# Second norm of the latent tiles between the context's q, k, v products; context pooling beside the latent projections

## The reference

```python
h = modulate(rms_norm(x, lp['g_ff1']), sh1, sc1)
x = x + 0.5 * g1 * swiglu(h, lp['w_ff1_in'], lp['w_ff1_out'])
h = modulate(rms_norm(x, lp['g_mix']), sh2, sc2)          # the second norm
proj = h @ lp['w_in']                                     # p, q, k, v and gate logits
q = rms_norm(q per head, lp['q_gain']); k = rms_norm(k per head, lp['k_gain'])
a = pool_mixer(p, lp['w_pool'], lp['pool_scale']) @ lp['w_br_pool']
b = attention(q, k, v) @ lp['w_br_att']    # context: dense; latent: 8x16 neighbourhood + cached keys
x = x + g2 * ((sig_A * a + sig_B * b) @ lp['w_out'])
h = modulate(rms_norm(x, lp['g_ff2']), sh3, sc3)
x = x + 0.5 * g3 * swiglu(h, lp['w_ff2_in'], lp['w_ff2_out'])
```

## Time and profile before

| | us |
|---|---|
| median of 3 runs | 1688.76 (1687.05 to 1701.29) |
| the profiled execution's own time | 1701.97 |
| its span on the slowest core (core 3) | 1700.4 |
| spans of the eight cores | 1680.7 to 1700.4 |
| PE busy, core 3 | 1536.0 (90%) |
| DVE, ACT, POOL busy, core 3 | 956.5, 494.2, 158.2 |

### The profile page before, as it was taken

How to read it: one execution, slowest core, us unless ns; L and a number is a source line. 1 busy time by engine, 2 the same in 40 slices (tenths; PEclk the granted TensorE clock), 3 DMA queues, 4 the chain that set the end, 5 groups by cost and what they waited for, 6 DMA issues and landing times.

```text
span 1700.4 us, 25281 instructions; the slowest of 8 cores (1680.7 to 1700.4 us)
## 1 busy us (share of the span) xinstructions
PE 1536.0 (90%) x8548; PEld 695.4 (41%) x8548; DVE 956.5 (56%) x1646; ACT 494.2 (29%) x739; POOL 158.2 (9%) x235
## 2 busy tenths in 40 slices
PE   1689999999999995698889888999999999999998
PEld 1234444444444442243434444444334444444443
DVE  2256556555566554464546665345366666666666
ACT  2651110111111125745636566235421111111110
POOL 2131000000000012300000000021210000000000
PEclk9799999999999997787889899999999999999999
DMA  9906442345432332457225355584322222222005
GB/s 183 243 1 91 75 67 37 48 74 76 75 48 43 59 87 99 101 116 142 37 56 120 99 113 113 138 186 75 50 38 38 37 38 38 38 38 38 13 1 198
DMA packets 35788, 134.68 MB, mean 79 GB/s; under 512 B 5072, under 2 KB 5200, under 8 KB 33616
## 3 DMA queue, kind: packets, MB, share of 16 engines
q0 software_dynamic: 22560, 79.88, 30.3%
q1 hardware_dynamic: 13104, 53.18, 9.3%
HBM read 191.95 MB, written 20.97 MB: 125 GB/s over the span
## 4 chain that ended last, share of the span: by engine, by line
PE 79%; DVE 6%; issue 5%; ACT 4%; DMA 4%; POOL 1%; DVEq 0%; ACTq 0%; SPq 0%; POOLq 0%
PE ps L413 76%; ACT arena L422 3%; DVE arena L430 3%; PE ps L410 3%; DMA arena<-wts 3%; DVE arena L426 2%; POOL arena L603 1%; DMA arena<-xin 1%; DVE arena L436 1%; ACT L422 1%; DVEq L183 0%; DVE arena L445 0%; DVE arena L442 0%; ACTq L183 0%; POOL arena L323 0%
## 5 line engine op out<-in xcount | busy, mean ns | idle before, releaser
L413 PE MATMUL ps<-arena 128*128 128x512 bf16 (+3 forms) x7108 | 1476.7, 363 | 132.9 <-DVE arena L430 53.5
L413 PEld LDWEIGHTS ps<-arena 128*128 128x128 bf16 x7108 | 646.7, 100 | 919.6 <-issue 336.8
L430 DVE SCALAR_TENSOR_TENSOR arena<-ps,arena 128x512 f32<-128x512 f32 (+2 forms) x860 | 562.5, 714 | 89.6 <-ACT arena L422 47.1
L422 ACT ACTIVATE arena<-ps 128x512 f32<-128x512 f32 (+4 forms) x418 | 266.1, 652 | 1045.8 <-PE ps L413 526.7
L426 DVE TENSOR_TENSOR arena<-arena,ps 128x512 bf16<-128x512 f32 (+1 forms) x198 | 130.2, 658 | 411.7 <-PE ps L413 382.4
L426 DVE TENSOR_TENSOR arena<-arena 128x512 f32<-128x512 f32 (+10 forms) x196 | 141.6, 738 | 114.9 <-ACT arena L422 89.3
L323 POOL DMA_DIRECT2D arena<-wts x150 | 79.9, 536 | 1255.5 <-PE ps L413 1025.0
L422 ACT ACTIVATE arena<-arena 128x512 bf16<-128x512 f32 (+6 forms) x230 | 165.6, 748 | 86.9 <-DVE arena L426 25.0
L410 PE MATMUL ps<-arena 128*128 128x65 bf16 (+3 forms) x1440 | 80.6, 214 | 25.5 <-DVE arena L436 16.0
L603 POOL TENSOR_TENSOR arena<-arena 128x512 bf16<-128x512 f32 (+3 forms) x77 | 75.9, 1010 | 186.4 <-ACT arena L422 99.3
L410 PEld LDWEIGHTS ps<-arena 64*128 64x128 bf16 (+1 forms) x1440 | 53.5, 98 | 79.0 <-issue 69.8
(11 more groups left out here) (12 smaller groups left out, 6.1 us busy)
## 6 DMA issues: line engine op xcount, KB each, us to landing
arena<-wts POOLq DMA_DIRECT2D x150, 512.0 KB, 8.8
arena<-xin SPq DMA_DIRECT2D x8, 1024.0 KB, 13.6
xspill<-arena SPq DMA_DIRECT2D x4, 2048.0 KB, 7.0
arena<-xspill SPq DMA_DIRECT2D x4, 2048.0 KB, 14.7
yoT<-arena SPq DMA_DIRECT2D x32, 256.0 KB, 2.3
arena<-ebias SPq DMA_DIRECT2D x12, 640.0 KB, 5.1
arena<-ebias SPq DMA_DIRECT2D x8, 768.0 KB, 5.4
nkT<-arena SPq DMA_DIRECT2D x8, 256.0 KB, 2.9
```

What stands on the lines that cost most here:

```text
L413: return P.emit("pe", lambda e: e.matmul(out, lhsT=lhsT, rhs=rhs, start=start, stop=stop), reads=reads, writes=writes, inc=inc)
L422: return P.emit("act", lambda e: e.activation(out=out, in_=in_, func=func, **kw), reads=reads, writes=writes)
L430: return P.emit("dve", lambda e: e.scalar_tensor_tensor(out=out, in0=in0, scalar=scalar, in1=in1, op0=op0, op1=op1), reads=reads, writes=w ...
```

## The change

Nothing is computed otherwise; instructions are issued in another order, on other engines and into other banks.

- The norms of tiles 2, 3 and 4 are no longer issued in stage I. `pump` stops at them, and `mixer` weaves all three between the context's q, k and v products (46 units of products against 78 pieces). All their squares go to POOL, and every second modulation to DVE (`sq="p"`, `mo="av"`). The norms of tiles 0 and 1 stay in stage I, with 6 of 8 squares on POOL and two pieces after a down product instead of three.
- For x of tiles 2 and 3 to stay in place during this, the memory is exchanged: context q, k, v now lie over x of tiles 0 and 1, latent k, v over tiles 2 and 3, and `x_reload` brings each tile back to the other pair's place.
- `p_gen(0)` moves from stage II to stage III, woven with the latent products.
- Banks: these norms' sums always take bank 4, so down products beside them, and in the last block of both feed-forward phases, rotate over three banks instead of four; the context products over four instead of six; the latent products over two (4, 5) instead of three, as bank 6 goes to `p_gen(0)`.

```diff
@@ build_program: order of the weight loads
-        for nm in ("q", "k", "p", "v"):
+        for nm in ("q", "k", "v"):
             plan_win(0, nm)
-        for nm in ("q", "k", "v"):
-            plan_win(1, nm)
+        plan_win(1, "q")
+        plan_win(0, "p")
+        plan_win(1, "k")
+        plan_win(1, "v")
@@ norm_stat, norm_gen
-        def norm_stat(tile):
+        def norm_stat(tile, bank=None):
-            b = poolB.next()
+            b = poolB.next() if bank is None else bank
...
-            b = stat if stat is not None else norm_stat(tile)
+            b = stat if stat is not None else norm_stat(tile, 4 if gap else None)
@@ ff_DN
-        def ff_DN(Dn, rd, nj, tile, hs, ig, ms=range(8), chunk_done=None):
+        def ff_DN(Dn, rd, nj, tile, hs, ig, ms=range(8), chunk_done=None, spare=False):
-                by = poolDN.next()
+                by = (poolDN3 if spare else poolDN).next()
...
         poolDN = PsumPool(P, [4, 5, 6, 7], "DN")
+        poolDN3 = PsumPool(P, [5, 6, 7], "DN3")
@@ ff_phase
             def pump(k):
-                while k > 0 and side:
+                while k > 0 and side and not (lazy_load is not None and side[0][0] > 1):
...
-                                  chunk_done=chunk_done if last else None)
-                            pump(3 if last else 2)
+                                  chunk_done=chunk_done if last else None, spare=bool(side) or last)
+                            pump(2)
@@ x_reload
-            claim_x(tt)
+            XT[tt] = XT0[tt ^ 2]
+            dst = XT[tt].rearrange("p c t -> p (c t)")
+            P.claim(oX[tt ^ 2], 16384, [("x", c, tt) for c in range(8)])
...
-        QT = (mem(oX[2], 8192, BF16, "p (h t) -> p h t", h=4), mem(oS, 8192, BF16, "p (h t) -> p h t", h=4))
+        QT = (mem(oX[0], 8192, BF16, "p (h t) -> p h t", h=4), mem(oS, 8192, BF16, "p (h t) -> p h t", h=4))
...
@@ mixer
-            while left and left[0][0] <= 2:
+            while left and left[0][0] < 2:
                 run_all(left.pop(0)[1])
...
-            d1, s1 = PsumPool(P, [0, 1, 2, 3, 4, 5], "d1"), PsumPool(P, [6, 7], "s1")
-            weave(qk_gen(0, "q", d1, s1), 16.0, side, 40.0)
...
-            weave(chain_gens(qk_gen(0, "k", d1, s1), v_gen(0, d1)), 30.0, p_gen(0, d1), 21.0)
+            d1, s1 = PsumPool(P, [0, 1, 2, 3], "d1"), PsumPool(P, [6, 7], "s1")
+            weave(chain_gens(qk_gen(0, "q", d1, s1), qk_gen(0, "k", d1, s1), v_gen(0, d1)), 46.0, side, 78.0)
...
-            d2, s2 = PsumPool(P, [4, 5, 6], "d2"), PsumPool(P, [7], "s2")
-            weave(chain_gens(qk_gen(1, "q", d2, s2), qk_gen(1, "k", d2, s2), v_gen(1, d2)), 54.0, ctx_att(), 32.0)
+            d2, s2 = PsumPool(P, [4, 5], "d2"), PsumPool(P, [7], "s2")
+            weave(weave_gen(chain_gens(qk_gen(1, "q", d2, s2), qk_gen(1, "k", d2, s2), v_gen(1, d2)), 54.0,
+                            p_gen(0, PsumPool(P, [6], "d2p")), 21.0), 75.0, ctx_att(), 32.0)
@@ ff1_tile_done
-            return norm_gen(1, TT_ALL[ti], sc="vvvp", gap=4)
+            if ti < 2:
+                return norm_gen(1, TT_ALL[ti], sq="pppa", sc="vvvp", gap=4)
+            return norm_gen(1, TT_ALL[ti], sq="p", sc="vvvp", mo="av", gap=4)
```

More of the change, by code:

```diff
@@ L823, in build_program @@
         SG = mem(oF, 8192, F32, "p (s t) -> p s t", s=4)
-        mrg_off = ([oX[2] + 8192 + 2048 * j for j in range(4)] + [oX[3] + 2048 * j for j in range(4)],
+        mrg_off = ([oX[0] + 8192 + 2048 * j for j in range(4)] + [oX[1] + 2048 * j for j in range(4)],
                    [oG + 2048 * j for j in range(8)])
@@ L1075, in pool_setup @@
             nb = NS * LP * 4
-            o_tb = oF if half == 0 else oX[3] + 8192
+            o_tb = oF if half == 0 else oX[1] + 8192
             if half == 0:
-                o_dt = [oX[3] + 8448, oX[3] + 10496]
+                o_dt = [oX[1] + 8448, oX[1] + 10496]
             else:
@@ L1231, in mixer @@
             P.claim(oS, 8192, [("qt", 1, hp, i) for hp in range(4) for i in range(8)])
-            P.claim(oX[2], 8192, [("qt", 0, hp, i) for hp in range(4) for i in range(8)])
-            P.claim(oX[2] + 8192, 8192, [("kt", 0, hp) for hp in range(4)])
+            P.claim(oX[0], 8192, [("qt", 0, hp, i) for hp in range(4) for i in range(8)])
+            P.claim(oX[0] + 8192, 8192, [("kt", 0, hp) for hp in range(4)])
+            P.claim(oX[1], 8448, [("vb", 0, i) for i in range(8)])
             P.claim(oG, 2048, [("sq", s) for s in range(2)])
```

37 lines of the change are left out of this document (18 added, 19 removed).

## The result

The changed kernel took **1727.32 us** in the median of its runs, the kernel before 1695.03 beside it: 1.0189 times as long, 95% interval 1.0115 to 1.0262. The profiled execution took 1716.86 us. Both medians count one much slower execution (1829.06 and 1823.58 us), which the ratio leaves out, and in two more runs of the changed kernel two or four cores were granted 0.941 to 0.946 over their span, where the others had 0.953 to 0.961, and took some 10 us or more longer. Measured again later (label e0_after), the same kernel took 1715.2 us against 1688.9, a ratio of 1.0154 (1.0134 to 1.0174). So the change costs 26 us, or 1.5%: slower, clear of noise in both measurements, where I had forecast no change and left 1722 as the end of the range.

What follows compares the result with a forecast made beforehand. TensorE, holding 79% of the chain, was taken to bound the kernel through idling and low clock. Terms of -20 - 5.6 + 29 + 2 = +5.4 us took the median from 1689 to 1694, range 1668 to 1722.

Steps and rivals of the forecast that it cites:

- A gain of 20 forecast: Stage I: two norms remain at 6.5 us each, so the loss falls from 33 to 13 us; bounds 12 to 23.
- If stage I keeps its waits of 4 us: Stage I: one of three stated signs that would show the forecast wrong, TensorE's waits of 4 us staying.
- I take 5 for a whole tile, 10 for two: Stage II: price of norms among context products, 10 us for two tiles, from 3 us seen for half a tile.
- my upper bound: Stage II: loss of 28 us, with each norm as dear as in stage I.
- A loss of 29 forecast: Stage III: its loss rises from 18 to 47 us through ring, VectorE, bank 6, tail and clock; bounds 19 to 53.
- The ring's waits, with VectorE's lateness: Stage III: products wait 25 us for a bank of two, plus 4 us where pooling additions delay the scaling.
- The term for bank 6: Stage III: bank 6 alone for p makes TensorE wait for ScalarE between a group's two small products, 2 us.
- goes to stage III: The pooling's wait at the end of stage II, 4.9 us, was said to move to stage III.
- the 25 us I worked out: Stage III: sum of waits for a free bank that p products, scores or values leave unfilled, 25 us.
- The rival of the low clock: Stage III: each 2 us wait slows the next product, clock costs 28.5 us instead of 10, total 1713; chance 0.33.
- Charging all 19 products: Stage III: the skill page's rule read as low clock for every product, 18 us more than the 10 us taken.
- Second feed-forward, memory exchange, weight order: Outside the three stages: down products over three banks cost 2 us (0 to 5); memory exchange and weight order nothing.

Runs made afterwards that it cites:

- e0_after: The changed kernel itself, nothing further changed, measured again later against the kernel before: 1715.2 us against 1688.9, ratio 1.0154.
- e8: The changed kernel with the scalings and modulations of tiles 2 to 4 left out (work omitted); stage II fell by 19 us.
- e7: The changed kernel with the modulations of tiles 2 to 4 all on VectorE instead of half on ScalarE; stage II grew by 2 us.
- e3: The changed kernel with p back in stage II and three latent banks, so the norms' move alone; stage I gives 24 us, stage II takes 30.
- e1: The kernel before with latent products on two banks instead of three, no norm or pooling moved; stage III grew by 45 us.
- e2: The kernel before with the pooling's move alone: p in stage III on bank 6, two latent banks; stage II 23.6 us shorter, III 50 longer.
- e5: The changed kernel with three latent banks and p on bank 7; stage III fell by some 21 us, excess over the kernel before 0.4%.

## Why the prediction was wrong, point by point

- **Stage I: the gain was right, in part by luck.** A gain of 20 forecast, 19 measured. The first context q product was to come 20 us earlier and came 24 us earlier, counted from the stage's mark; some 5 of these are sums of squares that moved to stage II. But the loss fell from 37.4 to 18.5 us, not from 33 to 13: both ends were some 5 us too low. One wait of 4.58 us and one of 3.18 remain, where I had worked out 3.6 in a norm. "If stage I keeps its waits of 4 us" was one of my signs of being wrong, and one such wait was kept.
- **Stage II: the step "I take 5 for a whole tile, 10 for two" failed.** Stages I and II together were to lose 25.6 us less and lose 15.4 less. Of the 21 us of loss in stage II, GpSimd's waits were 2.9 (4 forecast), which leaves the norms 18, not 11. I had read the price off a stretch with half a tile's norm, and had put it down to ScalarE having no room. e8 measures the price, 19 us of stage time for two tiles and the halo, and its source: scaling and modulation. e7 shows that moving ScalarE's share of them does not help. The 18 lies about midway between my 11 and my upper bound, each norm as dear as in stage I; e3, where stage II takes 30 us for the 24 that stage I gives, lies at that bound.
- **Stage III: the mechanism was right, two terms were short.** A loss of 29 forecast, 34.4 measured: 41.2 us idle (35.4 forecast) and 11.3 of clock (11.2). The ring's waits, with VectorE's lateness, were 26.1 us (29 forecast). The term for bank 6 was short: of the 7.4 us of waits for ScalarE 6.5 are for the copy of a mixing product out of bank 6, where I had 2. And one term was missing: I had written that the pooling's wait at the end of stage II "goes to stage III", and put nothing for it into the sum there; it is the 3.3 us ahead of the last mixing product. The stage took 139 to 142.6 us instead of "some 127"; the 83 I set out from had gone to 86 by its marks.
- **The two banks alone would have cost more than the sum shows.** e1 loses 41 us with no pooling there, and e2 is only 5 us longer. Of e1's 36.9 us of ring waits the p products fill some 11; the 25 us I worked out were right only with p in them. The other way round, e5 keeps the pooling there with a ring of three and still loses 15 us more in stage III than the kernel before. So of the 34 us the third bank gives 19 back, and 15 are left.
- **The clock.** 0.88 in stage III and 0.81 in e1. The rival of the low clock had 28.5 us for it. Its total, 1713, is 2 us from the second measurement and 14 from the first, but that is luck and not its mechanism: the clock took 11, and most of the rest is stage II. The rule of the Trainium skill ("TensorE: Matmul & The Clock Gate", "A second HAM failure mode: psum-queue depth-cycling") is borne out in direction: e1's waits, most of them around 2 us long, on a cycling ring go with a lower clock, 0.81 where the kernel before had 0.94, by the ring's size alone. Charging all 19 products, as I read it, comes to 28.5 us; e1, where all 19 wait, has 17 us, the changed kernel 11.
- **Second feed-forward, memory exchange, weight order:** +1 us by the part behind stage III, 2 forecast. No wait for a weight shows among those of the three stages.
- **The sum:** -15.4 + 34.4 + 1 = +20 on core 4, where +5.4 was forecast; 9 to 10 of the 15 us between are the step of stage II, 5 the terms of stage III. By its marks core 4 grew by 22.4 us over the three stages, 3 to 4 more than the losses say; busy time times clock is only roughly work. The slowest cores grew by 25, since stage II takes 71 or 73 us and III 139 to 142.6 by core, and the part behind adds 1. That makes the 26 measured.
- **The range.** The bounds of stage II (4 to 28) and III (19 to 53; the lower one is 17 by its own terms) both held what came, but the shifts added up. The first measurement lies 5 us above the end of the range, the second, 1715.2, inside it; a part of that is the cores with a lower clock in the first one. That the kernel would be no slower failed in both.

## What to carry to other kernels

A ring of PSUM banks has to be as long as the chain that frees a bank, counted in products and with everything that takes a turn in it. One bank less made a stage of 86 us 45 us longer here, and independent work woven in mostly hid waits that the smaller ring had made. Work moved beside other work was not free here, as its steps hand each other a buffer across two in-order queues that the host work also uses. Price such work by leaving out single steps and not by busy shares: all engines of stage II were below 81% busy. When work moves, move its waits in the sum too. When a wait has a name, take it away and look what name comes next before believing that it was the cost.

## What the runs showed that I had not expected

- Moving modulations off ScalarE, the engine TensorE waited for, made the stage longer (71 to 73 us before, 74.3 then).
- With the waits of stage II gone (2.5 us idle instead of 14.0) the granted clock there was 1.00 instead of 0.88: 7 of the 19 us of e8 are that.
- On GpSimd an addition of 128x1084 takes 1.99 us, of 128x1028 2.36; on VectorE 1.28 and 1.23.
